# Feed-forward in two phases: all gate and up slabs, then the down slabs with 512-column matmuls

## The chip, the cores and the metric

The kernel runs on one core of a Trainium2 chip. The metric is device time in microseconds of one execution, as the median over runs. A profiled execution gives the trace.

## The reference

A sequence of 256 tokens with 1024 features goes through three layers, each an attention part and a feed-forward part, all in fp32. The attention of the first layer is a mixture of stick-breaking and differential attention, that of the second has a forget gate (FOX), that of the third is a latent one (MLA). What matters here is the feed-forward part, which comes three times:

```
def swiglu(xn, w_gate, w_up, w_down):      # xn: 256 x 1024, inner width 2816
    return (jax.nn.silu(xn @ w_gate) * (xn @ w_up)) @ w_down
h = h + swiglu(rmsnorm(h, ffn_norm[l]), w_gate[l], w_up[l], w_down[l])
```

After the third one comes a last norm.

## The kernel before, in words

Everything is kept transposed, features on the 128 partitions and the 256 tokens along the free dimension. The residual `xT` is 8 chunks of 128 features.

**Weights.** They lie in HBM as slabs of 128 x 1024 fp32 numbers (512 KB), some 320 of them. SyncE loads slab after slab into the six slots of `stage`. Each is split in two fp32r parts: ScalarE copies it to `w_hi` (`split_hi`, line 1016, or `next_hi`, line 1032), VectorE writes the rest to `w_lo` (`split_lo`, `next_lo`, line 1485). A slot of `w_hi` and `w_lo` is free when TensorE has ended the slab (`slab_done`), a slot of `stage` when its low part is made (`lo_made`). ScalarE works six slabs ahead of TensorE, VectorE four.

**Products.** Activations are split in the same way, and three of the four products are formed: hi x hi, hi x lo and lo x hi. `by_weights` (line 428) does this with three matmuls of 256 columns for one block of 128 x 128 weights. `wide_slab` (line 753) keeps a_hi and a_lo side by side in `a_pair` and streams both, 512 columns, past the high weights, and 256 past the low ones. Half 0 of the bank then holds two of the products and half 1 the third; ScalarE copies half 1 to `low` (`low_out`, line 1219), and VectorE adds the two (`both_halves`, line 1688). Every matmul passes through line 426.

**Feed-forward.** A gate or up slab gives 128 of the 2816 inner features (8 blocks, one for each chunk of the input). Gate and up of the same features are a pair; there are 22. `silu(gate) * up` of a pair is split into `ff_hi` and `ff_lo`. A down slab takes one pair's 128 features to all 8 chunks of the output, accumulated in the eight halves of banks 0 to 3 (`acc`). A round of the loop holds six slabs: gate, up, down, gate, up, down, where a down slab uses the pair before the one just made. Banks 4 to 7 take gate and up slabs. The first two slabs of a block (`first_column_slabs`) go chunk by chunk as the norm's scaled input comes; then the norm's sum (`norm_sum`, on `ones`), two wide slabs, and the first down slab, which waits for `ff_lo` of the first pair (line 796). The loops of 9 rounds are hardware loops (`Fori`) on each queue, the last round is written out; in it the last up slab is a plain column slab into bank 7, and `last_rows` orders the last two down slabs so that chunks end early. `acc_done` tells VectorE that two more chunks are ready.

**Between the blocks.** For each chunk VectorE adds the bank to `xT` (`residual`, line 1515), ScalarE makes `a_hi` (line 1067) and the square (line 1053), VectorE `a_lo` (line 1504), GpSimd adds up the squares (line 2088). Behind the first feed-forward come FOX's slabs, behind the second the latent projections (`DQ`), whose results ScalarE and VectorE must have taken (`latlo_ready`) before the fifth of them starts, behind the third the sums of the last norm (`fin_squared`, `fin_added`) and the output.

## Time and profile before

| | |
|---|---|
| median of 3 runs | 1008.98 us (1008.75 to 1010.22) |
| span of the profiled execution, first to last instruction | 1007.6 us |
| matmuls recorded | 7214 |
| TensorE busy | 993.9 us, 99% |
| VectorE busy | 714.1 us, 71% |
| ScalarE busy | 607.8 us, 60% |
| GpSimd busy | 59.6 us, 6% |
| DMA | 174.05 MB, mean 173 GB/s |

The median is 1.4 us above the span; the page has no time of its own for what lies outside it. The times in the trace's views are microseconds from the start of the span. Matmuls overlap, so their durations can't be added up: a price is read from the distance of starts. `PEld` is TensorE's loading of weights, which goes on beside the matmuls. In the timeline a row can hold several equal instructions (x2), and then its duration is from the first one's start to the last one's end.

### The profile page before, as it was taken

Reading aid. Unit: us, or ns where it says so; the run is one execution under the profiler, and the core shown is the slowest. Engines: PE = TensorE matmul, PEld = TensorE weight load, DVE = VectorE, ACT = ScalarE, POOL = GpSimd, SP = SyncE. Lnnn points to the kernel's source line nnn. Section 1 sums busy time; section 2 is a strip of 40 time slices with the busy share of each in tenths; the row PEclk is TensorE's granted clock in tenths of the full one; section 3 lists DMA queues with packets and bytes.
Section 4 is the critical chain, followed back from the end, with each engine's and each line's share of the span. In section 5 each row is a group of like instructions: output and inputs, shape, how many; then the busy total and the mean of one; then the engine's idle time right before and its main releaser. Section 6 shows DMA issues by size and latency. Waiting matters only on the chain.

```text
span 1007.6 us, 19765 instructions
## 1 busy us (share of the span) xinstructions
PE 993.9 (99%) x7214; PEld 923.4 (92%) x7214; DVE 714.1 (71%) x1360; ACT 607.8 (60%) x1094; POOL 59.6 (6%) x79
## 2 busy tenths in 40 slices
PE   8999999999999999999999999999999999999997
PEld 8999989999999999989999999999989999999996
DVE  4668987776666668666496666668977686666665
ACT  5677785575555556565475555557768675555553
POOL 3011110120000002000020000002200010000000
PEclk9999999999999999999999999999999999999999
DMA  7743445466555554433545556564665456565631
GB/s 292 273 149 110 153 145 187 148 206 190 176 181 186 183 189 159 157 127 127 167 146 188 187 187 187 187 187 127 203 194 191 146 167 188 187 187 187 187 125 43
DMA packets 50904, 174.05 MB, mean 173 GB/s; under 512 B 6304, under 2 KB 8864, under 8 KB 50720
## 3 DMA queue, kind: packets, MB, share of 16 engines
q1 hardware_dynamic: 49664, 172.12, 52.9%
q10 hardware_dynamic: 1184, 1.18, 0.6%
q8 instruction: 36, 0.59, 0.2%
q14 instruction: 20, 0.16, 0.0%
HBM read 169.86 MB, written 1.05 MB: 170 GB/s over the span
## 4 chain that ended last, share of the span: by engine, by line
PE 90%; DVE 5%; ACT 2%; DMA 1%; issue 1%; SPq 0%; DVEq 0%; ACTq 0%
PE bank L426 89%; DVE w_lo L1485 2%; PE bank L647 1%; DVE a_pair L1504 1%; DMA stage<-slab_dram 1%; DVE xT L1515 1%; DVE arena L1478 0%; ACT w_hi L1032 0%; ACT a_pair L1067 0%; DVE soft_s L1566 0%; ACT soft_p L1124 0%; ACT w_hi L1016 0%; DVE tmp L1478 0%; DVE tmp L1712 0%; DVE arena_r L1485 0%
## 5 line engine op out<-in xcount | busy, mean ns | idle before, releaser
L426 PE MATMUL bank<-a_pair,w_hi 128*128 128x256 f32 (+1 forms) x1992 | 537.8, 342 | 2.8 <-DVE w_lo L1485 2.7
L426 PE MATMUL bank<-a_pair,w_lo 128*128 128x256 f32 x1488 | 417.6, 282 | 0.0
L1485 DVE TENSOR_TENSOR w_lo<-stage,w_hi 128x1024 fp32r<-128x1024 f32 (+2 forms) x322 | 387.4, 1211 | 8.4 <-ACT w_hi L1016 3.5
L426 PEld LDWEIGHTS bank<-a_pair,w_hi 128*128 128x128 f32 x1992 | 343.4, 190 | 48.6 <-DVE w_lo L1485 4.0
L426 PE MATMUL bank<-arena_r,w_hi 128*128 128x256 f32 x1792 | 328.8, 284 | 0.4 <-DVE arena_r L1485 0.2
L426 PEld LDWEIGHTS bank<-arena_r,w_hi 128*128 128x128 f32 x1792 | 278.4, 191 | 5.6 <-DVE arena_r L1485 1.4
L426 PEld LDWEIGHTS bank<-a_pair,w_lo 128*128 128x128 f32 x1488 | 283.1, 190 | 0.0
L426 PE MATMUL bank<-arena_r,w_lo 128*128 128x256 f32 x896 | 252.7, 283 | 0.0
L1016 ACT ACTIVATE w_hi<-stage 128x1024 fp32r<-128x1024 f32 x192 | 202.4, 1055 | 33.4 <-PE bank L426 33.4
L1032 ACT ACTIVATE w_hi<-stage 128x1024 fp32r<-128x1024 f32 (+2 forms) x126 | 128.0, 1026 | 79.5 <-PE bank L426 69.7
L426 PEld LDWEIGHTS bank<-arena_r,w_lo 128*128 128x128 f32 x896 | 171.0, 191 | 0.0
L1688 DVE TENSOR_TENSOR tmp<-bank,arena 128x256 f32<-128x256 f32 x123 | 51.9, 422 | 160.3 <-ACT arena L1219 160.3
L1219 ACT ACTIVATE arena<-bank 128x256 f32<-128x256 f32 x123 | 47.1, 383 | 163.2 <-PE bank L426 163.2
L2088 POOL TENSOR_TENSOR sumsq<-sumsq,sq 128x256 f32<-128x256 f32 x47 | 38.5, 820 | 644.3 <-ACT sq L1053 591.8
L1478 DVE TENSOR_TENSOR tmp<-tmp,rB 128x256 f32<-128x256 f32 x129 | 54.4, 422 | 4.8 <-ACT tmp L1210 2.7
L1214 ACT ACTIVATE arena_r<-tmp 128x256 fp32r<-128x256 f32 x66 | 27.6, 418 | 43.5 <-DVE tmp L1478 35.7
L426 PE MATMUL bank<-w_hi,a_pair 128*128 128x256 f32 x256 | 47.7, 287 | 0.0
L426 PEld LDWEIGHTS bank<-w_hi,a_pair 128*128 128x128 f32 x256 | 39.8, 191 | 0.9 <-issue 0.6
L426 PE MATMUL bank<-w_lo,a_pair 128*128 128x256 f32 x128 | 36.2, 282 | 0.0
L1566 DVE CUSTOM_DVE_ANT_0 soft_s<-bank,con 128x128 f32<-128x128 f32 x80 | 25.1, 355 | 15.5 <-PE bank L426 15.4
L1154 ACT ACTIVATE soft_p<-soft_s,small 128x128 f32<-128x128 f32 x64 | 31.2, 491 | 4.0 <-DVE small L1619 3.2
L1504 DVE SCALAR_TENSOR_TENSOR a_pair<-xT,vec,a_pair 128x256 fp32r<-128x256 f32 x48 | 28.7, 604 | 6.5 <-ACT a_pair L1282 5.1
(185 smaller groups left out, 674.8 us busy)
## 6 DMA issues: line engine op xcount, KB each, us to landing
stage<-slab_dram SPq DMA_DIRECT2D x319, 512.0 KB, 4.2
con<-con_dram SPq DMA_DIRECT2D x1, 1153.5 KB, 10.6
xT<-xT_dram SPq DMA_DIRECT2D x4, 256.0 KB, 5.5
arena<-arena ACTq DMA_DIRECT2D x1, 1024.0 KB, 8.9
arena<-tmp SPq DMA_DIRECT2D x32, 32.0 KB, 3.2
out_dram<-arena SPq DMA_DIRECT2D x3, 256.0 KB, 2.4
tmp<-arena SPq DMA_DIRECT2D x16, 16.0 KB
vec<-vec_dram SPq DMA_DIRECT2D x1, 213.5 KB, 11.5
```

The costliest lines, as they stand in the source:

```text
L426: return nc.tensor.matmul(out, lhsT, rhs, start=start, stop=True, skip_group_check=True)
L1016: nc.scalar.activation(w_hi[:, slot, :], stage[:, slot, :], ACT.Copy).then_inc(hi_made, 1)
L1032: nc.scalar.activation(hi, raw, ACT.Copy).then_inc(hi_made, 1)
L1154: last = nc.scalar.activation(soft_p[:, g % 2, cols], soft_s[:, g % 2, cols], ACT.Exp, scale=0.125 if g < HEADS else rq_col[:, t:t + 1], b ...
L1214: nc.scalar.activation(ff_hi[:, p, :], tmp[:, 4 + p, :], ACT.Copy).then_inc(ffhi_ready, 1)
L1219: nc.scalar.activation(low[:, i, :], half(4 + (0, 2, 1, 3)[i], 1), ACT.Copy).then_inc(low_taken, 1)
L1478: return nc.vector.tensor_tensor(out, a, b, ALU.mult)
L1485: return nc.vector.tensor_tensor(out, a, hi.bitcast(f32), ALU.subtract)
L1504: return nc.vector.scalar_tensor_tensor(out, x, g, hi.bitcast(f32), ALU.mult, ALU.subtract)
L1566: return nc.vector.tensor_tensor_reduce(out=s[:, cols], in0=b[:, cols], in1=con[:, mask + cols.start:mask + cols.stop], scale=1.0, scalar= ...
L1688: return nc.vector.tensor_tensor(out, half(b, 0), low[:, i, :], ALU.add)
L2088: nc.gpsimd.tensor_tensor(sumsq[:, :], sumsq[:, :], sq[:, (i % 2) * TOK:(i % 2 + 1) * TOK], ALU.add).then_inc(sq_added, 1)
```

## The change

The feed-forward of a block runs in two phases. First all 44 gate and up slabs, pair after pair, all but the first two slabs as wide ones; the pairs rotate over the banks (4, 5), (6, 7), (0, 1). All 22 pairs of `ff` are kept, hi and lo side by side: 20 in `arena`, which is free at that time, and 2 in `arena_r`. Then the 22 down slabs: a block of weights takes a pair's 512 columns with the high part and 256 with the low part, and each of the 8 output chunks has a whole bank. The first of them takes the chunks in an order by when their banks come free. The last four down slabs run chunk by chunk: chunk 0 of all four, then chunk 1, and so on, and each chunk is signalled when it is complete. The residual adds both halves of a bank, the low half first. `low` moves to `soft_t` and `soft_p`. The loops of SyncE, TensorE, ScalarE and VectorE are written out.

```diff
-        low = chunks(arena, 9216, 4)
-        ff_hi, ff_lo = chunks(arena_r, 0, 2), chunks(arena_r, 512, 2)
+        def ff_pair(q):
+            return span(ff_arena, 512 * q, 512) if q < 20 else span(arena_r, 512 * (q - 20), 512)
+        def ff_banks(q):
+            return ((4, 5), (6, 7), (0, 1))[q % 3]
+        DOWN_BANK = (4, 0, 1, 2, 3, 5, 6, 7)
+        DOWN_FIRST = (3, 4, 6, 7, 1, 2, 0, 5)
...
# SyncE
-                with sp.Fori(0, NG - 1) as i:
...
+                for j in range(DOWN + PAIRS):
+                    q = j // 2 if j < DOWN else j - DOWN
+                    of = 6 * (q // 2) + (2 * (q % 2) + j % 2 if j < DOWN else 4 + q % 2)
+                    load(base + j, base + of - first)
...
# TensorE
+            def down(d, c, slot, start):
+                out, w = bank[DOWN_BANK[c]], slice(c * P, c * P + P)
+                mm(out[:, :], w_hi[:, slot, w], ff_pair(d), start)
+                return mm(out[:, 0:TOK], w_lo[:, slot, w], ff_hi(d), False)
...
-                wide_slab(base + 2, (base + 2) % SLOTS, bank[6])
-                pe.wait_ge(r_ready, 2 * f + 2)
-                wide_slab(base + 3, (base + 3) % SLOTS, bank[7])
-                pe.wait_ge(fflo_ready, q + 1)
-                row_slab(base + 4, (base + 4) % SLOTS, *ff(0), True)
-                with pe.Fori(1, NG - 1) as i:
-                    ffn_round(f, base, i)
-                ffn_round(f, base, NG - 1, last=True)
+                for q in range(1, PAIRS):
+                    n, (of_gate, of_up) = base + 2 * q, ff_banks(q)
+                    if q >= 3:
+                        pe.wait_ge(gu_taken, q0 + q - 2)
+                    wide_slab(n, n % SLOTS, bank[of_gate])
+                    if q == 1:
+                        pe.wait_ge(r_ready, 2 * f + 2)
+                    elif q == 3:
+                        pe.wait_ge(ff_made, q0 + 1)
+                    elif q > 3:
+                        pe.wait_ge(up_taken, q0 - f + q - 3)
+                    wide_slab(n + 1, (n + 1) % SLOTS, bank[of_up])
+                free = {1: (gu_taken, q0 + 21), 2: (up_taken, q0 - f + 20), 0: (gu_taken, q0 + 22), 5: (up_taken, q0 - f + 21)}
+                for d in range(PAIRS - TAIL):
+                    n = base + DOWN + d
+                    pe.wait_ge(fflo_ready, q0 + d + 1)
+                    pe.wait_ge(lo_made, n + 1)
+                    for c in DOWN_FIRST if d == 0 else range(NC):
+                        if d == 0 and c in free:
+                            pe.wait_ge(*free[c])
+                        last = down(d, c, n % SLOTS, d == 0)
+                    last.then_inc(slab_done, 1)
+                pe.wait_ge(fflo_ready, q0 + PAIRS)
+                n = base + DOWN + PAIRS - TAIL
+                for c in range(NC):
+                    for i in range(TAIL):
+                        if c == 0:
+                            pe.wait_ge(lo_made, n + i + 1)
+                        last = down(PAIRS - TAIL + i, c, (n + i) % SLOTS, False)
+                        if c == NC - 1:
+                            last.then_inc(slab_done, 1)
+                    if c < NC - 1:
+                        last.then_inc(acc_done, 1)
...
# ScalarE
+                for q in range(1, PAIRS):
+                    n = base + 2 * q
+                    low_out(n, q, 0)
+                    ff_high(f, q - 1)
+                    next_hi(n)
+                    silu(q, gu_scaled, q0 - f + q)
+                    low_out(n + 1, q, 1)
+                    next_hi(n + 1)
...
+            def after_ffn(f, base):
+                norm_start(2 * f + 2)
+                for i in range(TAIL):
+                    next_hi(base + DOWN + PAIRS - TAIL + i)
...
# VectorE
+                for q in range(1, PAIRS):
+                    n = base + 2 * q
+                    gate(f, q)
+                    next_lo(n)
+                    ff_low(f, q - 1)
+                    silu_out(f, q)
+                    up(f, q)
+                    next_lo(n + 1)
+                for d in range(PAIRS - 2):
+                    next_lo(base + DOWN + d)
...
+                if m % 2 == 0:
+                    nc.vector.tensor_tensor(xT[:, c, :], xT[:, c, :], half(DOWN_BANK[c], 1), ALU.add).then_inc(low_added, 1)
+                    if between:
+                        between()
+                    dve.wait_ge(low_added, 8 * (m // 2 - 1) + c + 1)
+                nc.vector.tensor_tensor(xT[:, c, :], xT[:, c, :], out, ALU.add).then_inc(x_ready, 1)
```

## Rows read from the trace of the kernel before

**Rows 1.** The page: busy time by engine; the last chain's share by line.
```profile
PE 993.9 (99%) x7214; PEld 923.4 (92%) x7214; DVE 714.1 (71%) x1360; ACT 607.8 (60%) x1094; POOL 59.6 (6%) x79
...
PE bank L426 89%; DVE w_lo L1485 2%; PE bank L647 1%; DVE a_pair L1504 1%; DMA stage<-slab_dram 1%; DVE xT L1515 1%; DVE arena L1478 0%; ACT w_hi L1032 0%; ACT a_pair L1067 0%; DVE soft_s L1566 0%; ACT soft_p L1124 0%; ACT w_hi L1016 0%; DVE tmp L1478 0%; DVE tmp L1712 0%; DVE arena_r L1485 0%
```
**Rows 2.** The core's span and mean granted clock of TensorE.
```profile
core 0: 1007.6 us, clock 0.997
```
**Rows 3.** Timeline of TensorE, one loop round: start, duration, instruction. First matmul after each change of kind.
```profile
299.59 0.40 PE L426 MATMUL bank<-a_pair,w_hi 128*128 128x512 f32 x1
...
305.24 0.40 PE L426 MATMUL bank<-arena_r,w_hi 128*128 128x256 f32 x2
...
308.13 0.40 PE L426 MATMUL bank<-a_pair,w_hi 128*128 128x512 f32 x1
...
316.64 0.40 PE L426 MATMUL bank<-a_pair,w_hi 128*128 128x512 f32 x1
```
**Rows 4.** Timeline of TensorE: first of 384 branch and output matmuls, first feed-forward matmul.
```profile
153.25 0.40 PE L426 MATMUL bank<-arena_r,w_hi 128*128 128x256 f32 x2
...
199.33 0.28 PE L426 MATMUL bank<-a_pair,w_hi 128*128 128x256 f32 x1
```
**Rows 5.** Timeline of TensorE at the entries of the three blocks.
```profile
205.34 0.58 PE L426 MATMUL bank<-a_pair,w_hi 128*128 128x512 f32 x1
...
211.35 0.51 PE L426 MATMUL bank<-arena_r,w_hi 128*128 128x256 f32 x2
...
214.33 0.40 PE L426 MATMUL bank<-a_pair,w_hi 128*128 128x512 f32 x1
...
513.35 0.50 PE L426 MATMUL bank<-a_pair,w_hi 128*128 128x512 f32 x1
...
519.44 0.39 PE L426 MATMUL bank<-arena_r,w_hi 128*128 128x256 f32 x1 [0.18 <-DVE arena_r L1485]
...
816.05 0.53 PE L426 MATMUL bank<-a_pair,w_hi 128*128 128x512 f32 x1
...
822.14 0.50 PE L426 MATMUL bank<-arena_r,w_hi 128*128 128x256 f32 x2
```
**Rows 6.** Lines of VectorE in a half round; first gate product of the third block.
```profile
L1485 DVE TENSOR_TENSOR w_lo<-stage,w_hi 128x1024 fp32r<-128x1024 f32 x3 | 3.7, 1220 | 0.0
...
L1688 DVE TENSOR_TENSOR tmp<-bank,arena 128x256 f32<-128x256 f32 x2 | 0.8, 422 | 2.8 <-ACT arena L1219 2.8
...
819.32 0.41 DVE L1478 TENSOR_TENSOR tmp<-bank,rB 128x256 f32<-128x256 f32 x1
```
**Rows 7.** Lines of ScalarE in the same half round: busy us, mean ns, idle before.
```profile
L1016 ACT ACTIVATE w_hi<-stage 128x1024 fp32r<-128x1024 f32 x3 | 3.2, 1055 | 0.6 <-PE bank L426 0.6
L1219 ACT ACTIVATE arena<-bank 128x256 f32<-128x256 f32 x2 | 0.8, 383 | 2.8 <-PE bank L426 2.8
```
**Rows 8.** Timeline of VectorE and ScalarE, a chunk behind the first block.
```profile
389.83 0.41 DVE L1515 TENSOR_TENSOR xT<-xT,bank 128x256 f32<-128x256 f32 x1
390.17 0.63 DVE L1504 SCALAR_TENSOR_TENSOR a_pair<-xT,vec,a_pair 128x256 fp32r<-128x256 f32 x1
...
390.28 0.51 ACT L1067 ACTIVATE a_pair<-xT,vec 128x256 fp32r<-128x256 f32 x1
```
**Rows 9.** Timeline behind the second block: TensorE, ScalarE's two copies, VectorE's first latents.
```profile
695.88 0.28 PE L426 MATMUL bank<-a_pair,w_hi 128*128 128x256 f32 x1
...
702.30 0.38 PE L426 MATMUL bank<-a_pair,w_hi 128*128 128x256 f32 x1
...
699.89 1.99 ACT L1032 ACTIVATE w_hi<-stage 128x1024 fp32r<-128x1024 f32 x2
...
706.37 0.86 DVE L1504 SCALAR_TENSOR_TENSOR arena_r<-bank,vec,arena_r 128x256 fp32r<-128x256 f32 x2
```
**Rows 10.** Timeline of TensorE at the end: sums of the last norm.
```profile
998.59 0.59 PE L426 MATMUL bank<-sumsq,con 128*128 128x256 f32 x2
...
999.95 1.03 PE L426 MATMUL bank<-arena,con 128*128 128x256 f32 x4
```

252 lines of the change are left out of this document (85 added, 167 removed).

## The prediction

> **What bounds the kernel now.** Four views, in this order. First the busy times and the chain of work that ended last: TensorE is busy for 99% of the span, and nine tenths of the chain are matmuls of one helper, line 426 [rows 1]. VectorE (71%) and ScalarE (60%) sit beside it. So a change pays here only if it makes the stream of matmuls shorter, or takes out a place where TensorE stands still. Second the clock: 0.997 granted, which is the 2.4 GHz level for all but the first microseconds [rows 2]. Third the timeline of TensorE in a stretch of one feed-forward block where nothing stalls [rows 3]: this gives the price of a slab. Fourth the same timeline at the three places where a feed-forward block is entered, since that is where the stream has gaps [rows 5], and at the two places where it is left [rows 9, 10].
>
> The price of a slab. A gate or up slab is 8 blocks of a 512-column and a 256-column matmul; a down slab (and the slabs of the output projections) is 8 blocks of three 256-column matmuls. Both stream 768 columns per block. Branch and output slabs of the second kind stand back to back from 153.25 to 199.33: 46.08 us for 16 of them, 2.880 us each, 0.360 us a block [rows 4]. A round of the loop, 4 wide and 2 down slabs, takes 316.64 - 299.59 = 17.05 us [rows 3]. So a wide slab takes (17.05 - 5.76) / 4 = 2.823 us, 0.353 us a block. The difference, 0.057 us a slab, is two per cent, and this is nearly all that "512 columns instead of twice 256" has to give: the number of columns is the same.
>
> Here the Trainium skill has a rule (TensorE: Matmul & The Clock Gate, Back-to-back issue gap): a warm matmul costs its columns at 2.4 GHz plus about 2.5 ns, isolated. By that page one matmul less saves 2.5 ns a block, an estimate of 1.4 us for the whole change where the rows give 3.9. The rows do not agree with the 2.5 ns (a 256-column matmul takes 120 ns in them, the page gives 109), and I go by the rows.
>
> **The change part by part.**
>
> *Down matmuls with 512 columns.* 22 down slabs in each of 3 blocks, plus one up slab per block that ran as three 256-column matmuls a block (line 774) and is now a wide one: 69 slabs x 0.057 = 3.9 us saved. The trace has no 512-column matmul that changes its bank at every block. Bounds: the wide slab above (3.9 us, one bank throughout) and the down slab as it is (0: it goes through four banks, at 0.120 us a matmul like the column slabs, so changing the bank costs nothing there). I take 3.9, since the only difference between the two rows that the instruction has is its width. A loss has nothing in the rows.
>
> *The order: gate and up first.* What it removes is the wait for the first `ff` product. After the two first slabs of a block TensorE runs two wide slabs, 5.65 us by the price above, and then needs `ff_lo(0)`. It takes 211.35 - 205.34 = 6.01, 519.44 - 513.35 = 6.09 and 822.14 - 816.05 = 6.09 [rows 5]: 0.36 + 0.44 + 0.44 = 1.24 us standing still. The slab behind each wait takes 214.33 - 211.35 = 2.98 instead of 2.88, 0.1 us each, 0.3 in all. In the new order nothing on TensorE asks for that product for 42 slabs. What is late next is the reuse of banks: pair 3's gate wants pair 0's gate taken and its up slab wants `ff_made`. That product is finished about 5 us after the sum, and pair 3 begins four slabs, 11.3 us, after it. So 1.5 us are saved and no wait replaces them.
>
> *The load of VectorE in phase one.* This is the price of the order. Until now a round of three slabs (8.5 us) carries 3 splits and 6 small products on VectorE. In phase one a pair of slabs (5.65 us) carries 2 splits at 1.22 and the same 6 small ones at 0.42 [rows 6]: 2.44 + 2.53 = 4.97 us, 88% of the pair. ScalarE: 2 x 1.06 + 2 x 0.38 + 2 x 0.42 = 3.7 us, 66% [rows 7]. Followed through one pair from the end of slab n: ScalarE copies the low half (0.4), VectorE adds and scales (to 1.3), splits slab n+4 (2.5), makes `ff_lo` of the pair before and the product behind silu (3.3), by when ScalarE has copied the low half of slab n+1 (2.82 + 0.4); it adds, multiplies (4.2) and splits slab n+5 (5.4). It is ready before the next pair's 6.0. The split of slab n+4 is finished some 6 us before TensorE wants it. At the entry of a block the lead is smaller: VectorE comes out of the norm's splits and takes the first gate at about 3.4 us after the sum (819.32 against 816.05 in the third block [rows 5, 6]). By the same steps the fifth wide slab's split ends at about +7.7, and TensorE wants that slab at +11.3. The lead is 3.6 us and grows by about 0.7 us a pair. Cost: nothing, hidden under TensorE; the cover is that lead, and if VectorE needed more than 5.65 us a pair, each excess would be paid 63 times. Phase two is light: 1 split each for 2.82 us.
>
> *Code without loops.* Three loops of 9 rounds become straight code on all queues, SP's included: 66 loads a block are issued one by one, in the same order of waits. TensorE's 384 matmuls of [rows 4] are straight code already and stand at exactly 0.120 us. The turn of the loop shows no gap either: the two halves of a round, 299.59 to 308.13 and 308.13 to 316.64, take 8.54 and 8.51 us, and only one of them can hold the turn [rows 3]. Cost 0, gain 0; a loss is bounded by what straight code shows, nothing.
>
> *Handover from phase one to two.* The first down slab goes to eight banks, of which six were gate and up banks. Its order leaves the last pair's banks 4 and 5 for the end, 2.1 and 2.5 us into the slab. Bank 5 is free when the low half is copied and added: 0.2 + 0.38 + 0.42, about 1 us. No wait.
>
> *The last four slabs chunk by chunk, and the residual.* Before, TensorE left a block without a pause: at the second exit its matmuls go straight on at 695.88 [rows 9]. So the chunks' earlier sums have no pause to remove at this place. The residual now has two adds a chunk (both halves of a bank) where it had one: an add 0.41, the low part 0.63, the scaled copy on ScalarE 0.51 [rows 8]. The chunk's cycle becomes add, scaled copy, low part, about 0.41 + 0.51 + 0.5 = 1.45 us with the hand-overs, against 4 x 0.353 = 1.41 us that TensorE takes for a chunk. VectorE starts it late, about 1 us, as it first splits the second slab of the next stage; it ends about 2.3 us behind TensorE. The next stage's first two slabs ask for the last chunk only 4.6 us in. Hidden; it would cost from a cycle of about 1.8 us on.
>
> What moves: only two slabs of the next stage, instead of four, are split when the block ends, for the last four slots are all in use to the end. ScalarE makes four copies behind the norm where it made two. The third slab's copy is ready at about +4.1 and its low part at +5.3; it is wanted at 5.76 + 0.25 = +6.0 (after FOX's two first slabs even 1.8 us later, because of the forget gates). Slack 0.7 us. Behind the second block ScalarE is the tighter one: `latlo_ready` was given at 706.37 + 0.4 and wanted at 708.1 (702.30 + 5.76) [rows 9]. Two more copies (0.96 each, 1.99 for the pair [rows 9]) less an earlier end of the norm make it about 11.5 us after the block where it was 10.9, and it is wanted at 11.8. I book 0.2 us of loss, bounds 0 and 1.
>
> *The sum behind the second block.* From 695.88 to 702.30 are 6.42 us, where two slabs and a sum took 199.33 to 205.34 = 6.01 before [rows 4, 5, 9]: 0.41 us in which TensorE waits for GpSimd's squares. With a norm that is nearly done at the end of the block they come earlier. 0.4 us saved, bounds 0 and 0.4. At the entries from output projections nothing changes.
>
> *The end.* Four partial sums at 0.43 each and a fifth follow the last slab: 998.59 to 999.95 + 1.03 = 2.39 us [rows 10]. The chunk before last is now 1.4 us earlier, the last one has one add more (0.4). TensorE does four sums (1.7 us) while the last square is made (0.2 + 0.8 + 0.5 = 1.5), so it ends after about 2.3. Gain 0.1, bounds -0.3 and +0.2.
>
> **The sum.** 3.9 + 1.2 + 0.3 + 0.4 + 0.1 - 0.2 = 5.7 us. The profiled execution's span is 1007.6, so 1001.9 after; the median of the runs shown, 1008.98, lies 1.4 above the span and this stays: **1003.3 us**, 0.6% faster. About 0.2% (2 us) is what a measurement can tell from no change.
>
> **Rivals.**
> *A: the pace is not the wide one.* A down block of 512 columns pays for its change of bank, and stays at 0.360. For it: no row has that form. Against: a change of bank is free at 256 columns. It gives 1003.3 + 3.8 = 1007.1. Chance 0.07.
> *B: the handover bites.* Two prepared slabs instead of four, and two more copies on ScalarE. For it: slacks of 0.7 and 0.3 us worked out over ten steps. It costs 1 to 2 us at each of two exits: about 1005.5. Chance 0.12.
> *C, the other side: VectorE becomes the bound of phase one.* 4.97 us of 5.65 is small slack for an engine that waits for ScalarE four times a pair. It needs 5.65 + 0.09 a pair to eat the whole gain (63 x 0.09 = 5.7) and 5.65 + 0.12 to end slower by 0.2%. At 0.15 it is 1003.3 + 63 x 0.15 = 1012.8 us. Against: the walk above ends 0.6 us early, and instructions that follow without a wait start before the one ahead has ended, so 4.97 is too high rather than too low. Chance 0.05.
> *D: the clock falls in phase two.* All matmul records are at the 2.4 GHz level bar the start (mean 0.997 [rows 2]), and the down slabs go through four banks in them. Were the three down phases (62 us each) at 1.2 GHz, they would cost 186 us more, about 1189. The Trainium skill (TensorE: Matmul & The Clock Gate, A second HAM failure mode) reports such a swing for 512-column matmuls that cycle through banks with small idle gaps; the trace has neither gaps nor falls, and does not agree so far. Chance 0.01.
>
> **Numbers.** Forecast 0.75 (own range 1002.6 to 1004.3), A 0.07, B 0.12, C 0.05, D 0.01. Faster by over 0.2%: the forecast, B, and half of A, some 0.88; within: 0.06; slower: C and D, 0.06. The range reaches from the forecast's lower end, in which the sums of entry and end go well, over B: 1002.3 to 1006.
>
> **What would show it.** Right: matmuls of the down phase start in pairs 0.353 us apart; a block takes 5.76 + sum + 64 x 2.823, about 186.7 us from its first matmul to the next stage's in the first block, where it took 188.5; no gap over 0.2 us behind the second wide slab of a block. VectorE's idle time in phase one is 0.5 to 1 us a pair, before the add. Wrong: waits of TensorE for `w_lo` in phase one (C), for `w_lo` or for a latent at 6 to 12 us into DQ or FOX (B), down blocks 0.360 apart (A), a granted clock under 1 (D).

## The result and the profile after

The change makes the kernel faster, by 0.8%: 1001.42 us in the median of 4 runs (999.56 to 1002.82), against 1009.6 for the kernel before on the same chip (1008.75 to 1010.3). The ratio is 0.9917, interval 0.9906 to 0.9929. The forecast was 1003.3 with a range of 1002.3 to 1006; the gain is 8.2 us where 5.7 were forecast, so the direction holds, and the size of one term does not. The profiled execution took 1001.52 us, its span is 999.8.

The page after: busy times, the last chain by engine, and then the span with the granted clock. They answer to [rows 1] and [rows 2].

```profile
PE 986.7 (99%) x6662; PEld 894.1 (89%) x6662; DVE 731.0 (73%) x1387; ACT 595.7 (60%) x1097; POOL 58.2 (6%) x79
...
PE 95%; DVE 2%; ACT 1%; DMA 1%; issue 0%; SPq 0%; DVEq 0%; ACTq 0%
```

```profile
core 0: 999.8 us, clock 0.996
```

TensorE is still the bound, with 552 matmuls fewer (69 slabs x 8). The clock is where it was, so rival D is out: 512-column matmuls that take another bank at every block did not pull it down (a stretch of phase two stands among the windows below).

The timeline of TensorE after the change: for each feed-forward block its first wide matmul, its first down matmul, and the first matmul of what follows the block; between the second and third block also the norm's sum (x2: one fp32 matmul of the kernel, which the trace records as two) and DQ's next matmul.

```profile
205.19 0.58 PE L445 MATMUL bank<-a_pair,w_hi 128*128 128x512 f32 x1
...
321.86 0.39 PE L445 MATMUL bank<-ff_arena,w_hi 128*128 128x512 f32 x1
...
382.87 0.28 PE L445 MATMUL bank<-a_pair,w_hi 128*128 128x256 f32 x1
...
508.39 0.50 PE L445 MATMUL bank<-a_pair,w_hi 128*128 128x512 f32 x1
...
627.20 0.40 PE L445 MATMUL bank<-ff_arena,w_hi 128*128 128x512 f32 x1
...
689.39 0.28 PE L445 MATMUL bank<-a_pair,w_hi 128*128 128x256 f32 x1
...
695.15 0.59 PE L445 MATMUL bank<-sumsq,con 128*128 128x256 f32 x2
695.39 0.47 PE L445 MATMUL bank<-a_pair,w_hi 128*128 128x256 f32 x1
...
809.51 0.53 PE L445 MATMUL bank<-a_pair,w_hi 128*128 128x512 f32 x1
...
928.35 0.40 PE L445 MATMUL bank<-ff_arena,w_hi 128*128 128x512 f32 x1
...
990.54 0.59 PE L445 MATMUL bank<-sumsq,con 128*128 128x256 f32 x2
```

Read the three blocks side by side. The 42 wide slabs of phase one take 116.67, 118.81 and 118.84 us; the 22 down slabs of phase two take 61.01, 62.19 and 62.19. The second and third block agree with each other and with the forecast's price (62.19 / 22 = 2.827 us a slab, forecast 2.823). The first block is 3.3 us shorter for the same instructions, the same data sizes and the same clock: 61.01 / 22 = 2.773. This is where the unforeseen part of the gain lies. Measured from norm's sum to norm's sum, against the trace before, the first block gives 4.79 us, the second 1.55, the third 1.50, all that lies ahead of and between them 0.20, and the output takes 0.23 back: 7.8 in all, which is 1007.6 - 999.8.

The difference can be seen in single matmuls. The same kernel after, timeline of TensorE: five matmuls from phase one of the first block, then five of the second.

```profile
249.75 0.39 PE L445 MATMUL bank<-a_pair,w_hi 128*128 128x512 f32 x1
249.98 0.28 PE L445 MATMUL bank<-a_pair,w_lo 128*128 128x256 f32 x1
250.10 0.39 PE L445 MATMUL bank<-a_pair,w_hi 128*128 128x512 f32 x1
250.33 0.28 PE L445 MATMUL bank<-a_pair,w_lo 128*128 128x256 f32 x1
250.44 0.39 PE L445 MATMUL bank<-a_pair,w_hi 128*128 128x512 f32 x1
...
549.82 0.40 PE L445 MATMUL bank<-a_pair,w_hi 128*128 128x512 f32 x1
550.06 0.28 PE L445 MATMUL bank<-a_pair,w_lo 128*128 128x256 f32 x1
550.18 0.40 PE L445 MATMUL bank<-a_pair,w_hi 128*128 128x512 f32 x1
550.42 0.28 PE L445 MATMUL bank<-a_pair,w_lo 128*128 128x256 f32 x1
550.53 0.40 PE L445 MATMUL bank<-a_pair,w_hi 128*128 128x512 f32 x1
```

In the first block two blocks of weights take 250.44 - 249.75 = 0.69 us, in the second 550.53 - 549.82 = 0.71. By the trace's starts in nanoseconds, the distances in the first are 230 and 117 over and over (346.7 a block, 2.773 us a slab); in the second they repeat after three blocks: 233, 117, 241, 120, 236, 113 (353 a block). Call these the short and the long pace. Each is held for hundreds of matmuls. A slab of three 256-column matmuls has one pace alone, 120.0 each, 2.880 a slab.

Both paces were in the trace before. There, the timeline of TensorE behind the first block's sum, and in the loop round of [rows 3]:

```profile
208.65 0.39 PE L426 MATMUL bank<-a_pair,w_hi 128*128 128x512 f32 x1
...
209.34 0.39 PE L426 MATMUL bank<-a_pair,w_hi 128*128 128x512 f32 x1
...
300.65 0.40 PE L426 MATMUL bank<-a_pair,w_hi 128*128 128x512 f32 x1
...
301.36 0.40 PE L426 MATMUL bank<-a_pair,w_hi 128*128 128x512 f32 x1
```

Two blocks of weights took 0.69 at 208.65 and 0.71 at 300.65. The kernel before ran its first two wide slabs at the short pace, and all the later ones of that block, behind the first three-matmul down slab, at the long. The prediction knew only the average of [rows 3].

VectorE was the engine that the order loads most. The windows view of the kernel after (busy us and instructions of each engine, granted clock, DMA share, GB/s), 78 us of phase one and 45 us of phase two, both in the first block:

```profile
228.00:306.00 78.00, 78.00 (x452) 68.78 (x451) 65.23 (x114) 46.22 (x86) 0.00 (x0) 1.00 0.61 190
333.00:378.00 45.00, 45.00 (x261) 39.67 (x261) 21.56 (x24) 18.93 (x21) 0.44 (x1) 1.00 0.62 197
```

The engines stand in the order PE, PEld, DVE, ACT, POOL. 78 us are 14.06 pairs of 5.547, so VectorE is busy for 4.64 us a pair and ScalarE for 3.29. TensorE is busy for all 78. The granted clock is 1.00 in both phases.

### The profile page after: what moved, and what is told of

Read it like the earlier page. It is cut to its first block, busy times and chain, and to the rows that moved or that the text cites. A ratio compares the mean times of both kernels' runs of the same rounds, so it can differ in the third digit from the quotient of the medians.

```text
span 999.8 us, 17255 instructions
## 1 busy us (share of the span) xinstructions
PE 986.7 (99%) x6662; PEld 894.1 (89%) x6662; DVE 731.0 (73%) x1387; ACT 595.7 (60%) x1097; POOL 58.2 (6%) x79
## 4 chain that ended last, share of the span: by engine, by line
PE 95%; DVE 2%; ACT 1%; DMA 1%; issue 0%; SPq 0%; DVEq 0%; ACTq 0%
PE bank L445 94%; PE bank L672 1%; DMA stage<-slab_dram 1%; DVE w_lo L1490 1%; DVE arena L1483 0%; ACT w_hi L1058 0%; DVE soft_s L1580 0%; ACT soft_p L1150 0%; DVE soft_p L1608 0%; DVE arena L1834 0%; ACT arena L1073 0%; DVE arena L1867 0%; ACT arena L1072 0%; DVE soft_p L1604 0%; DVE arena L1832 0%
## 5 line engine op out<-in xcount | busy, mean ns | idle before, releaser
L445 PE MATMUL bank<-a_pair,w_hi 128*128 128x512 f32 (+1 forms) x1968 | 533.5, 343 | 2.0 <-DVE w_lo L1490 1.9
L1058 ACT ACTIVATE w_hi<-stage 128x1024 fp32r<-128x1024 f32 (+2 forms) x314 | 325.7, 1043 | 169.8 <-PE bank L445 159.5
L445 PE MATMUL bank<-ff_arena,w_hi 128*128 128x512 f32 x480 | 169.6, 396 | 0.0
L445 PE MATMUL bank<-arena_r,w_hi 128*128 128x256 f32 (+1 forms) x784 | 153.7, 293 | 0.0
L445 PE MATMUL bank<-ff_arena,w_lo 128*128 128x256 f32 x480 | 134.7, 281 | 0.0
L445 PEld LDWEIGHTS bank<-arena_r,w_hi 128*128 128x128 f32 x784 | 123.6, 191 | 3.7 <-issue 1.4
L445 PE MATMUL bank<-arena_r,w_lo 128*128 128x256 f32 x416 | 117.2, 282 | 0.0
L445 PEld LDWEIGHTS bank<-ff_arena,w_hi 128*128 128x128 f32 x480 | 90.0, 188 | 21.5
L445 PEld LDWEIGHTS bank<-ff_arena,w_lo 128*128 128x128 f32 x480 | 90.7, 189 | 0.0
L445 PEld LDWEIGHTS bank<-arena_r,w_lo 128*128 128x128 f32 x416 | 79.6, 191 | 0.0
```

The lines of the kernel that those rows point to most:

```text
L445: return nc.tensor.matmul(out, lhsT, rhs, start=start, stop=True, skip_group_check=True)
L1058: nc.scalar.activation(hi, raw, ACT.Copy).then_inc(hi_made, 1)
```

## Experiments

The theory at the start: the wide stream has two paces, a three-matmul slab sets the long one, and the change gains by keeping such slabs out of the block. The rival: only the width of the down matmuls counts, and the rest is scatter. Ratios are to the kernel before in the same batch. "S, L, L" gives the pace (short or long) behind the entry of the three blocks in the profiled execution. "One execution" means that the kernel's time is a single value; what is read there are the paces inside its trace.

### The same kernel again

> The changed kernel once more, unaltered. In its first trace the blocks of 512+256 columns stand 0.347 us apart in the first feed-forward and 0.353 us apart in the second and third. Theory T (chance): which cadence a feed-forward has is settled when its stream starts, after a wait of TensorE, and can differ from execution to execution; then this trace can show another set of blocks at 0.347, and the times spread by about 3 us (64 slabs x 0.047) for each block that differs. Theory P (place): the cadence belongs to the code or the data of a block; then it is again 0.347, 0.353, 0.353 and the time about 1001.4 us.

1000.5 us (998.34 to 1002.34, 6 runs), ratio 0.991 (0.9894 to 0.9926); the kernel before 1009.63. Profiled execution: S, S, L, span 997.5 where S, L, L gave 999.8. The runs spread over 4 us. A block at the other pace is 3.3 us, so the pace can account for the spread.

### Down slabs with three 256-column matmuls, all else as changed

```diff
-                mm(out[:, :], w_hi[:, slot, w], ff_pair(d), start)
+                mm(out[:, 0:TOK], w_hi[:, slot, w], ff_hi(d), start)
+                mm(out[:, TOK:2 * TOK], w_hi[:, slot, w], ff_lo(d), False)
```

> The changed kernel with each down block as three 256-column matmuls (hi x hi in half 0, hi x lo in half 1, lo x hi in half 0) into the same banks. It has the order of the change without its width. Prediction by its recorded terms: down slabs at 2.880 instead of 2.823, 66 x 0.057 = 3.8 us slower than the changed kernel. If down slabs of 512+256 run at 2.773 where the short cadence holds: 66 x 0.107 = 7.1 us with all three blocks short, 2.3 + 3.8 x 2/3 = about 4.9 us with one. Rival: the whole gain comes from the order, the width gives nothing: no difference. I expect phase one of the first block at 2.773 still, since no three-matmul slab precedes it.

1006.19 us (1003.97 to 1006.79), ratio 0.9961 (0.9948 to 0.9975), S, S, L in phase one. The width of the 66 down slabs is worth 1006.19 - 1000.5 = 5.7 us by the medians, where the prediction's price gives 3.8. The two profiled executions have the same paces, and their spans, 1002.8 and 997.5, differ by 5.3. The medians alone, with runs 3 to 4 us apart, would not shut out 3.8; the prices of a slab in the traces do: 22 x (0.107 + 0.107 + 0.053) = 5.9 us for S, S, L. The rest, 3.4 us against the kernel before, is all else that was changed, the short pace of phase one with it. The rival falls: phase one of two blocks is short here although the down slabs are what they were; what has changed for it is that they no longer stand between the wide slabs.

### One three-matmul slab in each phase one

The gate slab of pair 5 runs as three matmuls of 256 columns.

```diff
-            def wide_slab(n, slot, out):
+            def wide_slab(n, slot, out, three=False):
...
+                    if three:
+                        mm(out[:, 0:TOK], w_hi[:, slot, w], a_hi[:, k, :], k == 0)
+                        mm(out[:, TOK:2 * TOK], w_hi[:, slot, w], a_lo[:, k, :], False)
...
+                    wide_slab(n, n % SLOTS, bank[of_gate], three=q == 5)
```

> The changed kernel with one single slab per feed-forward (the gate slab of pair 5, the eleventh) as three 256-column matmuls a block; no wait is added. Theory S (slabs of three matmuls push TensorE into the long cadence, which then lasts): in the first block the slabs ahead of it stand at 2.773 and all behind it at about 2.82, 53 slabs x 0.047 = 2.5 us slower than a short block, as the kernel before had it after its first down slab. Theory W (a wait of TensorE with an empty queue does it): the slab itself costs 0.1 us and the cadence behind it is 2.773 as before; 0.3 us in all.

1004.56 us (1003.66 to 1006.28), ratio 0.9949 (0.9936 to 0.9962). In the first block the wide slabs ahead of it take 2.773 us, all behind it 2.827, down slabs too. The other two blocks were long from their entry and stayed so. The slab itself costs 0.1 us. The timeline of this kernel, first block, behind the slab of three:

```profile
231.04 0.40 PE L445 MATMUL bank<-a_pair,w_hi 128*128 128x512 f32 x1
231.28 0.28 PE L445 MATMUL bank<-a_pair,w_lo 128*128 128x256 f32 x1
231.40 0.40 PE L445 MATMUL bank<-a_pair,w_hi 128*128 128x512 f32 x1
231.63 0.28 PE L445 MATMUL bank<-a_pair,w_lo 128*128 128x256 f32 x1
231.75 0.40 PE L445 MATMUL bank<-a_pair,w_hi 128*128 128x512 f32 x1
```

It is the long pace (0.71 for two), in the block that is short in the kernel after. 24 matmuls of 256 columns in a row did it, and nothing turned it back for 50 slabs.

### The norm's sum three blocks into the first wide slab

```diff
-                norm_sum(2 * f + 1)
...
-                    wide_slab(n, n % SLOTS, bank[of_gate])
+                    wide_slab(n, n % SLOTS, bank[of_gate], (lambda: norm_sum(2 * f + 1)) if q == 1 else None)
```

The sum goes to bank 2, and the wait for `r_ready` ahead of pair 1's up slab goes.

> The changed kernel with the norm's sum moved three blocks of weights into the first wide slab of each feed-forward, and into bank 2, so that up slab of pair 1 need not wait for it. In blocks two and three TensorE then no longer stands still for 0.37 us at the sum, as the squares are added up by then. Theory W (waits at the entry set the cadence): all three blocks run at 2.773, and the time falls by 0.7 us of waits and 2 x 64 x 0.047 = 6.0 us, to about 994.7. Theory P (the cadence belongs to the block) or theory S: 0.7 us less and no more, about 1000.7.

999.21 us (996.35 to 1001.11), ratio 0.9894 (0.9876 to 0.9912); S, S, S with a span of 995.0. TensorE still stops: the first wide matmul comes 0.76 and 0.85 us after the one ahead in blocks two and three, released by `w_lo`. So the pause at these entries, which the expectation put down to the sum, is the wait for the first wide slab's low part, and moving the sum does not take it away. The median is 1.3 us under that of the same kernel without the edit, less than the spread of either. As a stop can leave either pace, S, S, S in one trace does not show that this edit brings it about.

### Single odd matmuls

Pair 5's gate slab is one of three again; at pair 8 stand, in the first block, a sum of 256 columns on `ones`, in the second one matmul of 128 columns into an idle bank (bank 3), in the third a wait.

```diff
+                    if q == 8:
+                        if f == 0:
+                            mm(half(3, 0), ones, sumsq[:, :], True)
+                        elif f == 1:
+                            pe.wait_ge(lo_made, n + 1)
+                            mm(bank[3][:, 0:P], w_hi[:, n % SLOTS, 0:P], a_hi[:, 0, 0:P], True)
+                        else:
+                            pe.wait_ge(ff_made, q0 + q - 1)
```

> The kernel with one three-matmul slab per feed-forward (pair 5), and three pairs later a probe ahead of pair 8's gate slab, another in each block, into a bank that phase one does not use. Block one: one fp32 matmul of 256 columns on the ones (as the norm's sum). Block two: one fp32r matmul of 128 columns. Block three: a wait of TensorE for the product of the pair just ended (it stands still for 1 us or more). All three blocks come to pair 8 in the long cadence (0.353 us). Theory R (the cadence is a matter of how the weight loads and matmuls stand to each other, and an odd matmul or a pause can set it anew): behind the fp32 matmul it is 0.347 again, as it is behind the norm's sum in the first block. If only a pause resets, block three alone changes, and if nothing does, all stay at 0.353 to the end of the block.

One execution of 1003.1 us. All three blocks were long behind the slab of three. The sum in the first block left the pace long. The 128-column matmul in the second turned it short to the end of the block. The wait in the third was over before TensorE came to it, so it tested nothing.

### The wait for the first product put back

TensorE waits for `fflo_ready` ahead of pair 2, and ScalarE and VectorE form that product where they did before.

```diff
+                    if q == 2:
+                        pe.wait_ge(fflo_ready, q0 + 1)
```

> The changed kernel with the removed wait put back: TensorE waits for ff_lo of the first pair ahead of the gate slab of pair 2, with ScalarE and VectorE making that part as early as the kernel before did. It undoes the order's one promised gain: 0.36 to 0.45 us of standing still in each block, 1.3 us in all, after the second wide slab. Theory T (a stop lets chance pick the cadence): at least one block changes its cadence at this wait; the first, which is at 0.347 in every trace so far, may go on at 0.353. Rival: a stop changes nothing, only slabs of three matmuls do; then each block keeps after the wait the cadence that it had ahead of it.

1003.66 us in one execution. At the wait the pace changes in all three blocks: short to long, long to short, short to long. A stop sets the pace anew. One slab's length across the stop, from the middle of pair 1's up slab to the middle of pair 2's gate slab, takes 3.161, 3.240 and 3.292 us, where half a slab of each pace would take 2.80. So the stops cost 0.36, 0.44 and 0.49. In the kernel before, the slab that ended at the stop and the one behind it were together 0.38, 0.45 and 0.41 over their paces.

### The last two down slabs chunk by chunk instead of four

```diff
-TAIL = 4
+TAIL = 2
```

> The changed kernel with only the last two down slabs chunk by chunk. A chunk then takes TensorE 0.70 us, and VectorE and ScalarE about 1.45 us. If my reading of the tail is right, they end about 6 to 7 us behind TensorE instead of 2.3, the next stage's first slabs ask for the last chunk 4.6 us in, and TensorE stands still for 1.5 to 3 us behind the first and second block; behind the third about 0.8 x 6 more for the last norm's chunks, 2 to 4 us. In all 5 to 9 us slower at equal cadence. Rival: the chunks are hidden anyway, no difference.

1011.18 us in one execution, S, L, L, span 1009.4: 9.6 longer than the kernel after at the same paces. The next stage's first two slabs take 8.64 and 8.53 us where they take 5.76, and the sum behind the second block has a gap of 0.91 instead of 0.24. That is 2.88 + 2.77 + 0.67 = 6.3 us; the end takes 1.1 more (10.35 us from the last norm's first sum to the end, 9.21 in the kernel after). What remains lies in front of the first block, where the edit changes nothing: its first wide matmul starts at 207.57 instead of 205.19. That stays open; the traces differ there by 1.7 us without an edit that could account for it (205.09 to 206.77, the kernel with a stop in each block left out). The timeline of this kernel behind the first block, the first matmul of three chunks of the next stage, each released by ScalarE:

```profile
388.42 0.38 PE L445 MATMUL bank<-a_pair,w_hi 128*128 128x256 f32 x1 [0.41 <-ACT a_pair L1093]
...
389.81 0.38 PE L445 MATMUL bank<-a_pair,w_hi 128*128 128x256 f32 x1 [0.41 <-ACT a_pair L1093]
...
391.20 0.39 PE L445 MATMUL bank<-a_pair,w_hi 128*128 128x256 f32 x1 [0.42 <-ACT a_pair L1093]
```

A chunk comes every 1.39 us, and TensorE alone would take 0.72. With two adds, the residual is a chain of 1.39 us a chunk (the prediction worked out 1.45). A tail of four slabs gives TensorE 1.39 us of work a chunk at the short pace and 1.41 at the long, and so keeps it busy beside that chain; a tail of two does not. A tail of three was not tried.

### Three-matmul slab, then one 128-column matmul, then another

```diff
+                    if q in (8, 14):
+                        pe.wait_ge(lo_made, n + 1)
+                        mm(bank[3][:, 0:P], w_hi[:, n % SLOTS, 0:P], a_hi[:, 0, 0:P], True)
+                    wide_slab(n, n % SLOTS, bank[of_gate], three=q == 5)
```

> One three-matmul slab at pair 5 of each feed-forward, and one fp32r matmul of 128 columns ahead of pair 8 and again ahead of pair 14. In one block of the run before, such a matmul turned 0.353 into 0.347 us. If it does so always, all three blocks are at 0.353 from pair 5 to 8 and at 0.347 behind, and the second one, which meets the short cadence, tells whether it turns it back (a toggle: 0.353 again) or leaves it (0.347 to the end). If the one case was chance, some of the three stay at 0.353 behind pair 8.

One execution, 1002.92 us. All three blocks entered short, were long behind the slab of three, short behind the first odd matmul, long behind the second. The timeline of the second block: ahead of pair 5, behind it, behind the first odd matmul, behind the second.

```profile
519.64 0.39 PE L445 MATMUL bank<-a_pair,w_hi 128*128 128x512 f32 x1
...
520.33 0.39 PE L445 MATMUL bank<-a_pair,w_hi 128*128 128x512 f32 x1
...
539.90 0.40 PE L445 MATMUL bank<-a_pair,w_hi 128*128 128x512 f32 x1
...
540.61 0.40 PE L445 MATMUL bank<-a_pair,w_hi 128*128 128x512 f32 x1
...
559.63 0.39 PE L445 MATMUL bank<-a_pair,w_hi 128*128 128x512 f32 x1
...
560.33 0.39 PE L445 MATMUL bank<-a_pair,w_hi 128*128 128x512 f32 x1
...
599.91 0.40 PE L445 MATMUL bank<-a_pair,w_hi 128*128 128x512 f32 x1
...
600.62 0.40 PE L445 MATMUL bank<-a_pair,w_hi 128*128 128x512 f32 x1
```

Two blocks of weights take 0.69, 0.71, 0.70 and 0.71; in nanoseconds the third is 694, as at the short pace. So one matmul of an odd length can turn the pace either way; within a block the same instructions on the same banks run at both, so the pace is a state of the stream, no property of the banks. In the four cases so far in which the odd matmul turned long to short, this one's three and the one above, it came at the same point of the three-block pattern: the two distances ahead of it were 232 or 233 and 117 or 118 ns.

### Two stops in each block, and nothing else

```diff
+                    if q in (8, 14):
+                        pe.wait_ge(ff_made, q0 + q)
```

> The changed kernel with two real stops of TensorE in phase one of each block: ahead of pairs 8 and 14 it waits for the product of the pair just ended, about 1.5 us each, 9 us in all. Theory T (each stop lets chance pick the cadence): of the nine stretches (entry to 8, 8 to 14, 14 to the block's end) some are at 0.347 and some at 0.353 in any order, with changes both ways at the stops and none between them. Rival: a stop always leads to one of the two.

One execution, 1009.67 us; TensorE stands still at each stop, 1.72 us from start to start where it is 0.12 otherwise, so with the slow restart a stop costs about 1.7 us. The paces at entry, behind the first stop and behind the second: S, S, S; L, L, S; S, L, L. A change comes only at a stop, in both directions, and not at each.

### Is the gain of the pace to be had for certain?

Two kernels force the long pace in blocks two and three with pair 1's up slab in three matmuls, and try to turn it with one 128-column matmul: directly behind that slab, or ahead of pair 4 (`q == 4` in place of `q == 2`). The kernel after ran again beside the first of them.

```diff
+                    if f and q == 2:
+                        pe.wait_ge(lo_made, n + 1)
+                        mm(bank[3][:, 0:P], w_hi[:, n % SLOTS, 0:P], a_hi[:, 0, 0:P], True)
...
+                    wide_slab(n + 1, (n + 1) % SLOTS, bank[of_up], three=f and q == 1)
```

> The changed kernel with the cadence of blocks two and three chosen rather than left to the stop at their entry: the up slab of pair 1 as three 256-column matmuls (this led to 0.353 us each time), then one fp32r matmul of 128 columns into an unused bank (this turned 0.353 into 0.347 each time). It costs 0.1 + 0.1 us a block. If both hold always, every execution has all three blocks at 0.347 us: from the 999.8 us span of the changed kernel's first trace (one block short) 6.0 us less and 0.4 more, 994.2, a median of about 996 with a spread under 1.5 us where the changed kernel's runs spread over 4.5. If the states are still drawn elsewhere, the spread stays and the median is near 1000.

> The changed kernel unaltered, beside the forced one on the same chip. Its block one at 0.347; blocks two and three by chance: times in steps of about 3 us between 996 (both short) and 1003 us (both long).

> As the forced kernel, with the 128-column matmul five wide slabs behind the three-matmul slab (ahead of pair 4) instead of directly behind it. There it followed 256-column matmuls and left 0.353 us; in the six cases where it turned the cadence it stood among 512+256 blocks that had settled. If that is the condition, all three blocks are at 0.347 from pair 4 on in each execution: the median is 1002.4 - 2 x 56 x 0.047 = about 997 us, with a spread of about 1 us. If not, 1002.4 again.

Directly behind: 1002.44 us (1001.74 to 1002.89), ratio 0.9929 (0.9915 to 0.9943), S, L, L. Behind a 256-column matmul the odd one did not turn the pace. But the spread is 1.15 us in five runs, where the unaltered kernel has 4.4 on the same chip (1001.07 us, 997.69 to 1002.11, ratio 0.9914, interval 0.9901 to 0.9928; S, S, L with a span of 996.0): with the pace held, most of the scatter goes. Not all of it need be the pace: the kernel with one slab of three is held long behind pair 5 too, and its six runs lie 2.6 us apart, on a chip where the kernel before spreads 3.9. Ahead of pair 4: 999.51 us (995.94 to 1000.17, 5 runs), ratio 0.9893 (0.9877 to 0.9909). The profiled execution was long in the second block even behind the odd matmul and short in the third, span 997.5; so my expectation of a sure switch failed once in two. (It speaks of five wide slabs between; there are four.) The two blocks were at different points of the three-block pattern when the odd matmul came: the distances ahead of it were 236 and 113 ns where the pace stayed long, 240 and 120 where it turned, and neither is the 233 and 117 of the four earlier cases. That the point in the pattern decides is argued, not shown.

### What leaves the entry open

The first block was short in all traces so far, and its first wide slab follows the sum without a stop, 0.03 us behind the start of the sum's last record. In blocks two and three there is a stop directly ahead of it: in the kernel after it follows 0.40 and 0.08 us behind that start. First the stops are put ahead of the sum; then, in a kernel of its own, a stop of over 1 us is put ahead of the first wide slab in each block.

```diff
                 first_column_slabs(base, [half(4, 0), half(5, 0)], 2 * f + 1)
+                if f:
+                    pe.wait_ge(lo_made, base + 3)
+                if f == 2:
+                    pe.wait_ge(sq_made, add_index(5) + 7)
                 norm_sum(2 * f + 1)
```

```diff
+                    if q == 1:
+                        pe.wait_ge(r_ready, 2 * f + 2)
                     wide_slab(n, n % SLOTS, bank[of_gate])
                     if q == 1:
-                        pe.wait_ge(r_ready, 2 * f + 2)
+                        pass
```

> In the second and third blocks the short waits at the entry (for the low part of the first wide slab, and in the third for the last square) stand ahead of the norm's sum, so that the first 512-column matmul follows the sum without a stop, as it does in the first block; nothing else differs, and the sum comes 0.2 to 0.7 us later. Theory: it is a stop directly ahead of a 512-column matmul that leaves it open which pace follows, and the first block runs at 2.773 us a slab in every trace because its first wide slab follows without a stop. Then all three blocks run at 2.773 us: span 994 to 996, time 996 to 998, and the values of the runs lie within 1.5 us. Rival: any stop at the entry draws the pace, wherever it stands: blocks two and three at 2.773 or 2.826 as before, time 998 to 1002 with a spread of 3 us or more.

> The same kernel again, for a second trace of it. Theory: all three blocks at 2.773 us a slab. Rival: at least one block of the second and third at 2.826.

> In each block the wait for the norm's inverse root stands ahead of the first wide slab instead of the second, so that TensorE stands still for about 1 us directly ahead of the first 512-column matmul, in the first block too; nothing else differs. Theory: each block's pace is drawn at this stop, and the first block can now be long as well; span 3 x 1 us longer than the same paces give without it, 997 to 1006. Rival: the first block is short for a reason that lies before the stop: it stays at 2.773 us.

The stop ahead of the sum: 1001.4 us (996.2 to 1004.27, 6 runs), ratio 0.9907 (0.9888 to 0.9926); its two traces are S, L, L (span 1002.5) and, in one more execution of 997.77 us, S, S, S (996.0). My theory fell, the rival holds: a stop some matmuls earlier leaves the pace as open. The stop in each block: 1008.46 us in one execution, and L, S, L. The timeline of that kernel in the first block:

```profile
208.71 0.50 PE L445 MATMUL bank<-a_pair,w_hi 128*128 128x512 f32 x1 [1.41 <-ACT rB L1065]
...
249.79 0.40 PE L445 MATMUL bank<-a_pair,w_hi 128*128 128x512 f32 x1
250.03 0.28 PE L445 MATMUL bank<-a_pair,w_lo 128*128 128x256 f32 x1
250.15 0.40 PE L445 MATMUL bank<-a_pair,w_hi 128*128 128x512 f32 x1
250.39 0.28 PE L445 MATMUL bank<-a_pair,w_lo 128*128 128x256 f32 x1
250.50 0.40 PE L445 MATMUL bank<-a_pair,w_hi 128*128 128x512 f32 x1
```

It is the only trace of 17 (both kernels and 15 experiments) in which the first block begins at the long pace, and the only one with a stop there. So the first block seems to be short, in 16 of 16 traces, because nothing stops TensorE between its 384 matmuls of branch and output slabs and the first wide one; that a stop there can leave it long rests on this one execution.

## Why the prediction was off

**The step that failed** is the price of a wide slab, "So a wide slab takes (17.05 - 5.76) / 4 = 2.823 us", and with it the term "Down matmuls with 512 columns". 2.823 is the long pace, within 0.004. It was taken as the only one, because it was an average over a round in which three-matmul slabs stand between the wide ones, and the removal of these is the change itself. Two things follow from the one error. The width of the down matmuls is worth 5.7 us by the medians of an experiment and 5.3 by two spans at equal paces, not 3.9: a down slab gains 0.053 at the long pace and 0.107 at the short. And the gate and up slabs, counted at no change, gain 0.05 each in a block that runs short, 42 x 0.05 = 2.1. One block at the short pace is 3.3 us, and the profiled execution has one. Without these the span would have been 999.8 + 3.3 = 1003.1, against a forecast of 1001.9. The first block is no luck, it was short in every trace without a stop ahead of it. What blocks two and three do is drawn at each execution: of the three traces of the changed kernel one is S, L, L with a span of 999.8, and two are S, S, L with 997.5 and 996.0. So a part of each single result is the draw; but even the slowest of these draws, S, L, L at 1001.52 us, lies under the range.

**The other terms** together were 1.2 us too favourable. Block two gave 1.55 and block three 1.50 where about 1.85 were forecast. Of the 0.3 and 0.35 that are missing, 0.2 is the price again: the long pace is 2.827 a slab and not the round's average of 2.823, over 62 slabs, wide and down. The rest is the stop, below. The output was 0.23 slower instead of 0.1 faster: TensorE's sums end 2.33 us after the last slab, as forecast, against 2.39 in [rows 10], and from the start of VectorE's last multiplies to the end of the span 5.8 us go by where it was 5.5. The multiplies themselves take 2.56 and 2.57, so the 0.3 lies behind them, and no experiment touched it.

**The entry stops** were real and no wait took their place. But they were over-priced: the 1.24 us read from [rows 5] for two wide slabs and the stop hold also the slow start of the first wide slab (2.96, 2.92 and 2.96 us), and that slab starts as slowly in the kernel after (2.96, 2.92 and 2.95). From the first wide matmul to the end of the second slab the kernel after is 0.28, 0.34 and 0.31 us quicker, 0.92 in all; with the 0.3 at the slab behind the stop the change took away 1.2 us, where 1.5 were booked.

**The handover** (rival B) did not bite. No stop of TensorE shows at 6 us into DQ. The sum behind the second block stands 0.24 ahead of its next matmul, 695.15 to 695.39, and the 0.4 us forecast there appear; but the reason given was wrong, and little of them is left. The prediction has TensorE wait for GpSimd's squares. In the trace before, the sum starts without a wait, at 701.65, and the pause is behind it. The timeline of TensorE there, and the waits of its weight loads from 700 to 703 us:

```profile
701.65 0.59 PE L426 MATMUL bank<-sumsq,con 128*128 128x256 f32 x2
702.30 0.38 PE L426 MATMUL bank<-a_pair,w_hi 128*128 128x256 f32 x1
...
PEld bank L426 <- DVE w_lo L1485: 0.5, 1, 0.5
```

So it waited for the third slab's low part, which the change makes earlier. Some 450 matmuls later, in the third layer's attention, TensorE waits for ScalarE in both kernels. The timeline before, then after:

```profile
755.46 0.52 PE L647 MATMUL bank<-con,soft_p 128*128 128x128 f32 x3 [0.61 <-ACT soft_t L1161]
...
748.94 0.52 PE L672 MATMUL bank<-con,soft_p 128*128 128x128 f32 x3 [0.92 <-ACT soft_t L1187]
```

From the sum to this matmul are 53.8 us in both, so what was won at the sum is lost here; from the sum behind block two to the sum ahead of block three the change gives 0.05 us. The experiment with a tail of two shows what the tail of four hides: some 6 us at the two exits.

**VectorE** (rival C) had more air than worked out: it is busy for 4.64 us a pair instead of 4.97, idle for 0.9 (forecast 0.5 to 1), and TensorE has no wait for `w_lo` inside phase one. That it also held at the short pace (a pair in 5.55) was needed for the larger gain.

**Banks** (rival A): down slabs of 512 and 256 columns have the same pace as the wide slabs ahead of them in every trace (62.19 / 22 = 2.827 us with a change of bank at each block, 2.827 without), so a change of bank at each 512-column matmul costs nothing.

**Straight code** cost nothing visible: no gap in either phase. The prediction weighed the 2.5 ns that the Trainium skill (TensorE: Matmul & The Clock Gate, Back-to-back issue gap) gives for a warm, isolated matmul beyond its columns, and went by the rows. The runs agree with that: one matmul less a block is worth 7 or 13 ns by the traces (360 less 353 or 346.7). An estimate from the page's 2.5 ns is 1.4 us for the width in the whole change; the width measured 5.3 to 5.7.

**The signs and chances.** The first block took 183.7 us from its first matmul to the next stage's where the prediction named 186.7, and down blocks there stood 0.347 apart instead of 0.353: both are the short pace. The chances as stated add up to 0.905 for a gain of over 0.2%, not 0.88.

What stays open: what in TensorE holds the pace, and what decides it at a stop. There is one hint. In the third block, where the entry's code is unaltered, the first wide matmul starts 69 or 70 ns after the last record of the sums in the four traces that went on short, and 67 or 77 to 87 ns after it in the nine that went on long (the kernel before among them). The second block does not bear this out: there the same distance, 402 ns, stands ahead of the long pace in the kernel after and of the short one in its second trace. So a few nanoseconds of the restart may take part in it, and what decides is not known. And no version here is surely better than the changed kernel: the lowest medians, 999.21 and 999.51, lie inside its spread.

## What to carry to other kernels

Read a price from single starts in more than one place of the trace before it is multiplied by 69. An average over a mixed round holds for that mixture only: if a change takes one kind of instruction out from between the others, look in the trace for a stretch where they already stand alone, be it two slabs long. A stop read from the distance of starts holds the slow restart behind it as well: look whether that stays when the wait goes. When the new kernel's runs scatter more than the old one's (4.4 us against 1.8 on one chip), compare stretches with the same instructions inside one trace, then ask what separates them.

## What the runs showed of the hardware

A stream of fp32r matmuls, 512 and 256 columns by turns, each with its own weights, has two lasting paces at the same granted clock: 346.7 and 353 ns for the two. A stop of TensorE sets it anew, either way; a slab of 256-column matmuls with a wide slab directly behind it leaves the long one (in all 11 blocks where such a slab was put in). In the first block, the sum on `ones` (two records) stands between the 256-column slabs and the wide ones, and the pace is short; with the sum moved three blocks on, the distances are 233, 117, 242, 119, 236 up to it and 230 and 117 behind it. But a sum put into a long stretch at pair 8 left it long (one case). A single 128-column matmul turned long to short in 4 of 4 cases with five wide slabs between it and the slab of three, in 1 of 2 with four, and in 0 of 2 directly behind; a second one, 12 slabs after the first, turned short to long in 3 of 3. 256-column matmuls alone keep to 120.0 ns. On this kernel one pace against the other is 3.3 us a block, more than the stops that the change was to remove (1.2 us in all).
